# Four cached keys in each of 32 partitions: another layout for the pages of a paged cache

## The reference, cut to what matters

```python
k_past = cache_k[l, page_table].reshape(bs, past, N_HEADS, 2, QK_HEAD)
v_past = cache_v[l, page_table].reshape(bs, past, N_HEADS, V_HEAD)
s = jnp.einsum('bqhcd,bkhcd->bhcqk', q, k) * (QK_HEAD ** -0.5)
p = softmax(s); a = p[:, :, 0] - lam * p[:, :, 1]
o = jnp.einsum('bhqk,bkhd->bqhd', a, v)
```

## Time and profile before

| | |
|---|---|
| median of 3 runs | 2385.55 us |
| span of the profiled execution | 2380.2 us |
| mean granted TensorE clock | 0.916 |
| TensorE matmul busy | 1984.2 us, 83% |
| VectorE busy | 1056.3 us, 44% |
| ScalarE busy | 486.3 us, 20% |
| GpSimd busy | 354.0 us, 15% |
| moved by DMA | 404.21 MB |
| attention stage, first page issued to last value product | about 430 to 1304 us |

### The profile page before, as it was taken

One profiled execution on the slowest core, in us unless ns is written; L12 is line 12 of the kernel. 1 busy time (PEld: TensorE's weight loads), 2 busy tenths in 40 slices (PEclk: granted clock), 3 DMA queues, 4 the chain that ended last, 5 costly groups with the idle time before them and its releaser, 6 DMA issues.

```text
span 2380.2 us, 47877 instructions
## 1 busy us (share of the span) xinstructions
PE 1984.2 (83%) x17492; PEld 1635.0 (69%) x17492; DVE 1056.3 (44%) x1528; ACT 486.3 (20%) x831; POOL 354.0 (15%) x544
## 2 busy tenths in 40 slices
PE   4699999668786876878785794999999997999992
PEld 1277898557665765767674793777777776888881
DVE  2424211666675665766561557111111112455457
ACT  0300111021212112121221203111211111333331
POOL 0000000223242423324232104200000000000003
PEclk7799999799897988889796896999999998999996
DMA  9711223779897979879896410121212123411112
GB/s 302 256 36 35 72 71 118 250 245 341 285 385 282 385 279 346 314 283 381 298 354 234 156 35 18 54 71 53 88 53 70 53 88 128 137 41 37 36 32 91
DMA packets 210968, 404.21 MB, mean 170 GB/s; under 512 B 24426, under 2 KB 88938, under 8 KB 210788
## 3 DMA queue, kind: packets, MB, share of 16 engines
q1 hardware_dynamic: 161012, 261.51, 31.9%
q0 software_dynamic: 41488, 136.35, 15.5%
q10 hardware_dynamic: 8320, 4.19, 0.6%
HBM read 377.53 MB, written 24.51 MB: 169 GB/s over the span
## 4 chain that ended last, share of the span: by engine, by line
PE 65%; DVE 13%; SPq 7%; DMA 7%; issue 6%; ACT 1%; DVEq 0%; ACTq 0%
PE psum L753 26%; PE psum L1002 11%; PE psum L761 10%; PE psum L852 5%; DVE k_turned L1432 4%; SPq L445 4%; SPq L449 3%; DMA ada_w<-w_ada 3%; DMA k_ring<-cache_k 3%; PE psum L1009 2%; PE psum L862 2%; DVE p_t L424 2%; PE psum L736 2%; PE psum L832 1%; DVE x_lo L1282 1%
## 5 line engine op out<-in xcount | busy, mean ns | idle before, releaser
L852 PE MATMUL psum<-k_turned,q_blocks 128*32 128x128 f32 x4096 | 332.3, 286 | 85.6 <-DVE k_turned L1432 84.9
L852 PEld LDWEIGHTS psum<-k_turned,q_blocks 128*32 128x32 f32 x4096 | 291.7, 114 | 137.1 <-issue 98.5
L1432 DVE STREAM_TRANSPOSE k_turned<-k_ring 128x2048 f32<-128x2048 f32 x128 | 295.4, 2308 | 6.6 <-DMA k_ring<-cache_k 5.7
L753 PE MATMUL psum<-x_hi,w_hi 128*128 128x512 f32 x896 | 281.3, 395 | 0.0
L753 PE MATMUL psum<-x_lo,w_hi 128*128 128x512 f32 x896 | 277.3, 391 | 0.0
L753 PE MATMUL psum<-x_hi,w_lo 128*128 128x512 f32 x896 | 276.0, 389 | 0.0
L1301 DVE TENSOR_TENSOR w_lo<-w_raw,w_hi 128x2048 fp32r<-128x2048 f32 x37 | 86.9, 2350 | 363.1 <-ACT w_hi L1057 353.5
L1002 PE MATMUL psum<-d_hi,h_hi 128*128 128x256 f32 x704 | 209.2, 297 | 12.2 <-DVE d_lo L1646 11.1
L862 PE MATMUL psum<-v_ring,p_t 128*32 128x128 f32 x4096 | 191.7, 295 | 19.3 <-DMA v_ring<-cache_v 18.9
L1002 PE MATMUL psum<-d_lo,h_hi 128*128 128x256 f32 x704 | 199.9, 284 | 0.0
L1002 PE MATMUL psum<-d_hi,h_lo 128*128 128x256 f32 x704 | 199.7, 284 | 0.0
(11 more groups left out here) (228 smaller groups left out, 2525.1 us busy)
## 6 DMA issues: line engine op xcount, KB each, us to landing
k_ring<-cache_k SPq DMA_DIRECT2D x256, 256.0 KB, 8.0
k_ring<-cache_k POOLq DMA_DIRECT2D x256, 256.0 KB, 6.1
v_ring<-cache_v SPq DMA_DIRECT2D x256, 256.0 KB, 8.8
v_ring<-cache_v POOLq DMA_DIRECT2D x256, 256.0 KB, 6.0
ada_w<-w_ada SPq DMA_DIRECT2D x12, 2048.0 KB, 9.6
w_raw<-w_in SPq DMA_DIRECT2D x12, 1024.0 KB, 5.3
w_raw<-w_gate SPq DMA_DIRECT2D x11, 1024.0 KB, 5.4
w_raw<-w_up SPq DMA_DIRECT2D x11, 1024.0 KB, 6.3
```

What stands on the lines that cost most here:

```text
L753: last = mm(psum[:, 2 * ft + c, 0:CH], w[:, s, k, ft * P:(ft + 1) * P], x[:, k, c * CH:(c + 1) * CH], start=k == 0 and j == 0, stop=k == K ...
L852: last = mm(psum[QUAD * h:QUAD * (h + 1), g % 2, 0:GP * QUAD], q_blocks[:, h, d, :], k_turned[:, g % 2, :, h * HD + d * QUAD:h * HD + (d + ...
L1432: v.transpose(k_turned[:, g % 2].rearrange("p j n -> p (j n)"), k_ring[:, g].rearrange("p j n -> p (j n)")).then_inc(k_free, 1)
```

## The change

The destination and the source of the page DMA are seen differently. Nothing else changes: the number of DMAs, their bytes, order, queues, semaphores and all compute are the same.

```diff
-                    eng.dma_start(ring[:, g, j, :], pages[ds(page, 1)].rearrange("o p d -> p (o d)")
+                    eng.dma_start(ring[QUAD * j:QUAD * (j + 1), g].rearrange("p s d -> p (s d)"),
+                                  pages[ds(page, 1)].rearrange("o (p s) d -> p (o s d)", s=z.PAGE // QUAD)
                                   ).then_inc(landed[g], 16)
```

## The result

The changed kernel takes 2726.43 us (median of 4 runs, 2704.60 to 2736.72), the kernel before 2384.47 on the same chips (4 runs). The ratio is 1.1424 (95% interval 1.137 to 1.1479), so 342 us or 14% slower. Forecast were 2742 us and +357.

What follows compares the result with a forecast made beforehand. TensorE and VectorE were taken to pace the stage, DMA a few per cent behind; at 225 GB/s DMA takes over, stage end 1661 against 1304. That +357 us added to the median gives 2742 us, range 2380 to 2880.

Steps and rivals of the forecast that it cites:

- turning point at 325 to 330 GB/s: Page-loading stage: DMA rate a step needs; above it the step keeps its time, below it DMA sets the time.
- Rate of 32 partitions: Page DMAs into 32 partitions: 225 GB/s taken, ends 206 and 282, so DMA becomes the bound; likeliest case, 0.50.
- The nearest row: Trace of the kernel before: ada_bias load, 768 KB into 32 partitions, 225 GB/s with DMA engines 0.94 busy.
- the correction for its repeated source: ada_bias load: its pieces all read the same 24 KB; allowing a factor of 0.85 for that gives 282 GB/s.
- Gain by longer pieces: Page DMAs: 8 KB rows would run at 425 GB/s against 386 for 2 KB, 10% of the DMA rate.
- The faster rival: Page loads: no limit of partitions, stage stays with TensorE and VectorE; about -8 us, 2377 us, at best 2361; chance 0.20.
- DMA without a gap: Stage: freed slots keep loads running between steps, so 275.20 MB at 225 GB/s take 1223 us, ending at 1661.
- The first step: Start of the stage: only keys wanted, about 20 MB or 89 us in place of 93 us of compute; 4 us idle.
- the account by steps: Stage counted by steps: 152 us for 105, +47 for each of seven, tail 56 for 46; about 340 us.
- Clock at no cost: TensorE in the stage: even at the lower clock a step's work takes about 126 us, under 152; no cost.
- Rival of overlapping halves: Two queues' pages in opposite halves half the time: 291 GB/s, +80, 2465 us; narrow for part of the time, 0.17.
- The waits of SP and POOL for a free slot gone: Issuing queues in the stage: a sign expected in the changed profile, no size given.

Runs made afterwards that it cites:

- long128: Changed kernel with one 1 MB DMA per group, 8 KB into each of 128 partitions, pages in pool order (not the reference's attention); 2368.95 us, ratio 0.9933.
- step2: Changed kernel with each page sent to every second of all 128 partitions, 4 KB in each, in one of two column blocks; 2377.18 us, ratio 0.9963.
- step4: Changed kernel with each page sent to every fourth of all 128 partitions, 32 partitions with 8 KB each; 2373.87 us, ratio 0.9957.
- slot0: Kernel before with only slot 0's groups, a quarter of the pages, sent to 32 partitions as in the changed kernel; 2569.88 us, ratio 1.0788.
- spqueue: Kernel before with only SP's half of the pages sent to 32 partitions as in the changed kernel; 2691.20 us, ratio 1.1297.
- keys32: Changed kernel with only keys sent to 32 partitions; values go to all 128 as in the kernel before; 2716.09 us.
- opposite: Changed kernel with page order altered so each queue alternates between partition halves and the two queues stand in opposite halves; 2693.37 us.
- short32: Changed kernel with pieces of 2 KB again, each page still going to 32 partitions in a row; 2765 us.

## Why the prediction was right, and where it was not

- **Bound of the kernel before, and the turning point at 325 to 330 GB/s.** In their full windows long128, step2 and step4 moved 408, 389 and 385 GB/s and lost nothing; slot0, spqueue and keys32 moved 298, 259 and 244 and lost 187, 308 and 330 us; and the kernels in which each page lies in one half moved 219 to 239 over the stage and lost 279 to 382 us. The turning point lies between 298 and 382; nothing was run between, so 325 to 330 itself is not tested.
- **Rate of 32 partitions, 206 to 282, taken 225.** Measured 225 over the stage, single windows 207 to 258. The nearest row, one load of 768 KB, carried it; the correction for its repeated source (282) was not needed. That the two agree to the digit is partly luck: the 225 of that load stood at share 0.94 and was not brought to full share, though the sum has DMA without a gap. At full share it is 239, and the sum gives 2670 us. The upper end of the range, by the same sum at 206, is 2855, not 2853.
- **Gain by longer pieces, 425 GB/s.** Right in sign; 408 in long128, with other DMAs too, and from 382 and not 386, which was one window of 5 us. The faster rival had 8 us for it and 24.6 at best; long128 gained 14.
- **DMA without a gap, sum 430 + 1223 + 4 + 4 = 1661.** The last value products were done at 1654.6 us, where the last `o_scaled` starts. A step was forecast at 152 us and took 150.7; the tail at 56, and took 61. The first step was put at no loss and lost some 20 us: its softmax begins at 538.7 us, and at 518.2 before. Up to there 22.8 MB had moved (108 us at 211 GB/s), where the forecast had 20 MB at 225. The sum had all bytes of the stage in it and did not rest on this; the account by steps did, and came out short by it, at 340 us.
- **Clock at no cost.** The mean fell from 0.916 to 0.872, the work of a step grew to 99 us at the most, under the 150.7.
- **Rival of overlapping halves, +80.** Not so; opposite won 33 us back, a tenth of the loss, where this rival wanted over 260.
- **The waits of SP and POOL for a free slot gone: wrong.** POOL's wait for key slots went up, from 182.5 us to 411.7, and SP's from 184.5 to 395.3. I had thought that with slow loads slots would always be free. But issuing a page takes a queue 1.2 us (4.86/4) and its transfer at half of 225 GB/s 2.3: the queues run ahead until all four slots are ordered, and then wait, as before, until one has landed and been used. A full ring of orders is what keeps the engines busy. The sum did not rest on this.
- **"Times" of a mixture.** In the rival of overlapping halves I took the mean of two pages' times at the narrow and at the full rate (2.33 and 1.27 us). The three runs with a mixture show that adding times so is too kind: in full windows 298 GB/s where it gives 327, 259 and 244 where it gives 284.

## What to carry to other kernels

Look at which partitions one DMA reaches before looking at how long its pieces are: 8 KB in place of 2 KB brought at most 0.7% here, and a destination inside one half of the partitions cost 12 to 16%. If a long piece needs few partitions, lay them with a step over all 128 (step4, 0.4% faster than the kernel before), as long as the consumer doesn't care for the order, and look at what the stepped form costs the issuing queue. When a load bounds nothing yet, work out the rate at which it would: here the margin was some 15% of 386 GB/s, and no destination in one half came near it.

## What the runs showed that I had not expected

A minority of narrow transfers is enough: a quarter of the pages costs over half of the full loss, and pages of the other queue that go to all partitions land in 19.5 us for 6.1. Of two queues with the same bytes, the one with the smaller packets landed later (21.8 us against 11.2 in short32, 19.5 against 10.7 in spqueue). An SP issue of the same 256 KB takes 315 ns (32 partitions in a row), 333 (128), 472 (32 with a step of four) or 478 (64 in a row, half of the slot's columns); what in the form sets it was not isolated.
